# A mixture-of-experts stage kept in slot order: the finish stage removed, its norm moved into the expert loop, and the routing done in batches

## The reference

```python
scores = jax.nn.sigmoid((t @ router_w).astype(jnp.float32))
biased = (scores + router_bias).reshape(-1, 4, 4)          # 4 groups of 4 experts
group_score = jnp.sum(lax.top_k(biased, 2)[0], axis=-1)
sel_group = jnp.argmax(group_score, axis=-1)               # one group a token
_, local_idx = lax.top_k(in_group, 2)                      # two experts in that group
gate = gate / jnp.sum(gate, axis=-1, keepdims=True)
for e in range(16):
    h = jax.nn.silu(t @ w_gate[e]) * (t @ w_up[e])         # 1024 -> 256
    y = y + combine[:, e:e + 1] * (h @ w_down[e])          # 256 -> 1024
x = layer_norm(alpha * x + y, ln_moe_g, ln_moe_b)          # alpha = 2 ** 0.25
```

## Time and profile before

| | us |
|---|---|
| median of 3 runs (lowest, highest) | 1128.58 (1125.63, 1130.79) |
| the profiled execution | 1127.5 |
| its span, first to last instruction | 1125.7 |
| PE busy | 986.8 (88%) |
| DVE busy | 531.6 (47%) |
| ACT busy | 368.3 (33%) |
| POOL busy | 183.5 (16%) |

### The profile page before, as it was taken

One profiled execution on the slowest core, in us unless ns is written; L12 is line 12 of the kernel. 1 busy time (PEld: TensorE's weight loads), 2 busy tenths in 40 slices (PEclk: granted clock), 3 DMA queues, 4 the chain that ended last, 5 costly groups with the idle time before them and its releaser, 6 DMA issues. The chain is left out here.

```text
span 1125.7 us, 15349 instructions
## 1 busy us (share of the span) xinstructions
PE 986.8 (88%) x5513; PEld 843.3 (75%) x5513; DVE 531.6 (47%) x1056; ACT 368.3 (33%) x717; POOL 183.5 (16%) x242
## 2 busy tenths in 40 slices
PE   7999999998999997999999999824999999999700
PEld 6898786766778876888768888724999999999600
DVE  6724513776666655455535454561332333323138
ACT  5112212434443435010132333201355443553331
POOL 0022100211000000112100000002233232332246
PEclk9999999998999999999999999955999999999955
DMA  8102010003500003602300000037698898988376
GB/s 313 55 29 75 1 57 1 1 1 141 235 1 1 1 1 141 232 1 75 101 15 19 20 20 38 38 96 228 191 273 275 253 280 264 282 280 236 56 146 190
DMA packets 57734, 131.24 MB, mean 117 GB/s; under 512 B 8912, under 2 KB 11216, under 8 KB 57680
## 3 DMA queue, kind: packets, MB, share of 16 engines
q1 hardware_dynamic: 49360, 100.95, 26.0%
q0 software_dynamic: 8320, 29.56, 11.7%
HBM read 103.14 MB, written 27.34 MB: 116 GB/s over the span
## 5 line engine op out<-in xcount | busy, mean ns | idle before, releaser
L1606 PE MATMUL h_ps<-xgT,e_gate_up 128*128 128x192 f32 x1024 | 172.0, 330 | 2.1 <-DVE xgT L1681 2.1
L1606 PEld LDWEIGHTS h_ps<-xgT,e_gate_up 128*128 128x128 f32 x1024 | 170.1, 193 | 3.4 <-issue 2.3
L238 PE MATMUL unit_ps<-whi,xhi 128*128 128x512 f32 (+1 forms) x256 | 98.1, 383 | 9.5 <-DVE wlo L269 9.5
L239 PE MATMUL unit_ps<-wlo,xhi 128*128 128x512 f32 (+1 forms) x256 | 97.7, 382 | 0.0
L240 PE MATMUL unit_ps<-whi,xlo 128*128 128x512 f32 (+1 forms) x256 | 97.5, 381 | 0.0
L719 PEld LDWEIGHTS o_ps<-mla_v,prob_T 128*128 128x128 f32 x576 | 72.1, 195 | 15.6 <-issue 10.6
L1691 DVE TENSOR_TENSOR e_dn_lo<-e_dn_raw,e_dn_hi 128x512 fp32r<-128x512 f32 x64 | 39.9, 686 | 84.7 <-ACT e_dn_hi L1641 58.7
L698 PE MATMUL s_ps<-mla_kT,mla_qT 96*128 96x512 f32 (+3 forms) x192 | 73.2, 507 | 3.4 <-PEq L1990 3.4
L719 PE MATMUL o_ps<-mla_v,prob_T 128*128 128x64 f32 x576 | 72.0, 276 | 2.9 <-ACT prob_T L754 2.7
L238 PEld LDWEIGHTS unit_ps<-whi,xhi 128*128 128x128 f32 x256 | 48.4, 189 | 17.9 <-DVE xlo L308 7.3
L240 PEld LDWEIGHTS unit_ps<-whi,xlo 128*128 128x128 f32 x256 | 48.5, 189 | 7.8
(11 more groups left out here) (293 smaller groups left out, 1884.6 us busy)
## 6 DMA issues: line engine op xcount, KB each, us to landing
e_gate_up<-w_gu SPq DMA_DIRECT2D x128, 256.0 KB
e_dn_raw<-w_dn SPq DMA_DIRECT2D x64, 256.0 KB, 5.1
wraw<-w_in SPq DMA_DIRECT2D x24, 256.0 KB, 4.7
y_rows<-zeros SPq DMA_DIRECT2D x10, 512.0 KB, 14.7
xraw<-xT SPq DMA_DIRECT2D x8, 512.0 KB, 6.9
w_out_raw<-w_out SPq DMA_DIRECT2D x8, 512.0 KB, 6.5
x<-x SPq DMA_DIRECT2D x8, 512.0 KB, 6.6
x_rows<-x SPq DMA_DIRECT2D x8, 512.0 KB, 2.6
```

The lines of the kernel that those rows point to most:

```text
L238: pe.matmul(o, hi, whi[:, s, 0:w], start=(s == 0), stop=False)
L239: pe.matmul(o, hi, wlo[:, s, 0:w], start=False, stop=False)
L1606: end = pe.matmul(o, gate_up[:, b, s, w], xT[:, s, :], start=(s == 0), stop=(s == GU - 1))
```

## The change

- A slot is a place in one table of 16 x 192 rows: the expert in the order in which they run, and the token's number in it. The experts run in another order (`RUN`): the first of each of the four groups, then the second of each, and so on. A token's two experts are in one group, so their steps lie at least four apart.
- Routing moves into `cross_attend`, in three batches of tiles: 0 to 3, 4 and 5, 6 and 7 (`rank_experts`, `choose`, `place`, `number`). The sigmoid becomes an exponential on ACT (L1228) and add and reciprocal on DVE. The second set of matmuls is gone. `describe` makes for every slot a weight (already divided by alpha), the token's other slot and the token's number.
- POOL scatters each tile's rows twice, to both slots of a token, into `xs_dram` (16 indirect DMAs, `scatter`, L1442), and at the head of `experts` 16 small ones of 16 bytes a row into `info_dram` (L1574). SP then loads the rows of an expert as one plain piece of the table (`fetch`), two steps ahead, then the slots' data (`info`) and the gains; DVE waits for the gains and POOL's constants before it begins its first step (`consts_made`, `gains_loaded`).
- In a step DVE makes `z = weight * result + row` out of PSUM with the row sum (L1750). SP stores z in slot order in `z_dram`. For a token's second slot, POOL has first gathered the first slot's z over the row (`gather_low`, L1597; lists entries out of bounds are skipped). Mean, the sum of squares (ACT, L1712), 1/sqrt (POOL, L1617) and the norm (DVE, L1760 and, in the next step, `put_out`, L1729) follow in the loop, and POOL scatters finished rows straight to the output (L1620), then waits until they have landed before it goes on.
- The transposed rows are copied by ACT alone (L1681, L1682), and the weights are loaded in one DMA for each of the two kinds. Experts 0 and 1 have their gate and up weights, and expert 0 its down weights, loaded in `cross_attend`.
- `attend` now writes 25.2 MB of zeros (two tables of 3072 rows). `route` and `finish` are gone; `overflow` norms and stores by itself when it runs.

```diff
+SLOTS = NE * CAP
+RUN = [g * EG + e for e in range(EG) for g in range(NG)]
 ...
-            for t in range(NT + 2):
-                sp.dma_start(k.y_dram[t * P:(t + 1) * P, :], zeros[:, 0:D]).then_inc(k.rows_zeroed, 16)
+            for t in range(SLOTS // P):
+                sp.dma_start(k.xs_dram[t * P:(t + 1) * P, :], zeros[:]).then_inc(k.rows_zeroed, 16)
+                sp.dma_start(k.z_dram[t * P:(t + 1) * P, :], zeros[:]).then_inc(k.rows_zeroed, 16)
 ...
     cross_attend, DVE:
+                if t == NT:
+                    choose(0)
 ...
+                if t == NT:
+                    number(0)
                 if t:
                     residual(t - 1)
+                if t == NT - 1:
+                    rank_experts(0)
-            copy_logits(NT - 2)
             norm(NT - 1)
-            copy_logits(NT - 1)
+            rank_experts(1)
+            choose(1)
+            rank_experts(2)
+            number(1)
+            choose(2)
+            number(2)
+            for n in range(3):
+                describe(n)
 ...
     cross_attend, POOL, after the last tile's 1/sqrt:
+            def scatter(n):
+                pool.wait_ge(slots_made, n + 1)
+                for t in range(*BATCHES[n]):
+                    for j in range(2):
+                        pool.indirect_dma_start(k.xs_dram, IndirectOffsetOnAxis(ap=k.slot[:, t, j:j + 1], axis=0), x1[:, t, :], None, ...)
 ...
     experts, SP:
+            sp.wait_ge(k.rows_scattered, 16 * 2 * NT)
+            for e in range(2):
+                fetch(e * CAP, e)
+            sp.wait_ge(k.info_scattered, 16 * 2 * NT)
+            for c in range(2):
+                sp.dma_start(info[0:ROWS[c], :, c, :], slots[c * P:c * P + ROWS[c]]).then_inc(info_loaded, 16)
+            sp.dma_start(g[:], over(A["ln_moe_g"], [P, D])).then_inc(k.gains_loaded, 16)
 ...
+                hold(z_stored, n(32, 128))
+                for c in range(2):
+                    hold(z_made, n(4, 2 * c + 6))
+                    sp.dma_start(k.z_dram[bass.ds(n(CAP, c * P), ROWS[c]), :], z[c][:]).then_inc(z_stored, 16)
+                if not isinstance(e, int):
+                    fetch(n(CAP, 2 * CAP), b)
 ...
     experts, POOL, a step:
-                for c, (_, rows) in enumerate(blocks):
-                    hold(y_taken, n(4, 2 * c + 6))
-                    pool.indirect_dma_start(k.y_dram, ..., yo[c][...], None, compute_op=ALU.add).then_inc(y_added, 16)
-                pool.wait_ge(y_added, n(32, 32))
+                if not last:
+                    hold(z_made, n(4, 4))
+                    read_info(n(1, 1), 1 - b)
+                    hold(ids_read, n(1, 2))
+                    hold(z_stored, n(32, 64))
+                    hold(rows_t, n(1, 2))
+                    gather_low(1 - b)
+                hold(squared, n(2, 2))
+                pool.tensor_scalar(sq[:], sq[:], 1.0 / D, EPS / ALPHA ** 2, ALU.mult, ALU.add)
+                hold(out_made, n(2, 2))
+                pool.tensor_tensor(rs[:], sq[:], half[:], ALU.pow).then_inc(rstd_made, 1)
+                for c in range(2):
+                    hold(out_made, n(2, c + 3))
+                    pool.indirect_dma_start(A["out"], ..., o[c][:], None, ...).then_inc(out_scattered, 16)
+                hold(out_scattered, n(32, 32))
+                pool.sem_inc(out_free, 1)
 ...
     experts, DVE, a step, after h and its low part:
+                put_out(n)          # waits rstd_made and out_free; o = tmp * rs + b
+                dve.wait_ge(low_gathered[b], h(32, 32))
+                dve.wait_ge(z_stored, n(32, 128))
+                for u, (c, j) in enumerate(UNITS):
+                    dve.wait_ge(ysum, n(4, u + 9))
+                    dve.scalar_tensor_tensor(z[c][:, f], yps[r, BANK[u], :], wgt[...], rows[b][c][:, f], ALU.mult, ALU.add,
+                                             accum_out=zsum[r, c, j:j + 1]).then_inc(z_made, 1)
+                # two means, two of tmp = (z - mean) * g, then the next expert's low parts
```

More of the change, by code:

```diff
@@ new lines, in cross_attend @@
+    st = at("ln2_st", 201.5, [P, 2, 6])
+    mv = at("ln2_mv", 201.625, [P, 2, 2])
+    rs = at("ln2_rs", 201.75, [P, 2])
+    half = at("ln2_half", 201.875, [P, 1])
+    nmx = at("xneg_max", 202, [P, XH])
+    rsum = at("xrow_sum", 202.0625, [P, XH])
+    rinv = at("xrow_inv", 202.125, [P, XH])
+    rb = at("router_bias", 24, [P, NE])
+    ones = at("ones", 24.25, [P, P], bf16)
+    tri = at("up_to", 24.5, [P, P], bf16)
+    neg_exp = at("neg_exp", 24.75, [P, NT, NE])
+    score = at("score", 25.25, [P, NT, NE])
@@ L1102, in logits, with place @@
                 last.then_inc(logit, 1)
+            def place(n):
+                lo, hi = BATCHES[n]
+                pe.wait_ge(chosen, n + 1)
+                if n == 0:
+                    pe.wait_ge(consts_made, 3)
+                    pe.wait_ge(exps, XH * NT)
+                o = sps[:, n % 2, 0:NE * (hi - lo)]
+                last = pe.matmul(o, tri[:], sel_b[:, lo:hi, :].rearrange("p t e -> p (t e)"), start=True, stop=(hi == 1))
+                for t in range(hi - 1):
+                    first = max(t + 1, lo)
+                    last = pe.matmul(sps[:, n % 2, NE * (first - lo):NE * (hi - lo)], ones[:],
+                                     over(sel_b[:, t:t + 1, :], [P, hi - first, NE]), start=False, stop=(t == hi - 2))
+                last.then_inc(placed, 1)
             def outputs(t):
@@ L1149, in _ @@
                 logits(t)
+            place(1)
+            place(2)
+            pe.wait_ge(ov_made, 1)
+            pe.matmul(ops[0:1, 0:1], ovsum[:], ones[:, 0:1], start=True, stop=True).then_inc(ov_sum, 1)
         @block.scalar
@@ L1230, in norm, with rank_of @@
                 dve.wait_ge(x2_made, t + 1)
-            def copy_logits(t):
-                dve.wait_ge(logit, t + 1)
-                dve.tensor_copy(k.logits[:, t, :], qps[:, 0:NE]).then_inc(lg_copied, 1)
+            def rank_of(out, b, v):
+                n = v.shape[1]
+                for j in range(4):
+                    if j < 3:
+                        last = dve.tensor_tensor(b[:, j, :, j + 1:4], over(v[:, :, j:j + 1], [P, n, 3 - j]), v[:, :, j + 1:4], ALU.is_ge)
+                    if j:
+                        last = dve.tensor_tensor(b[:, j, :, 0:j], over(v[:, :, j:j + 1], [P, n, j]), v[:, :, 0:j], ALU.is_gt)
+                link(last)
+                link(dve.tensor_reduce(out, b.rearrange("p j n i -> p n i j"), AX.X, ALU.add))
@@ new lines, in experts @@
+    rows = [[at(f"x_rows{b}{c}", 44 + 8 * c + 4 * b, [ROWS[c], D]) for c in range(2)] for b in range(2)]
+    z = [at(f"z{c}", 60 + 4 * c, [ROWS[c], D]) for c in range(2)]
+    tmp = [at(f"ln3_tmp{c}", 68 + 4 * c, [ROWS[c], D]) for c in range(2)]
+    o = [at(f"ln3_out{c}", 76 + 4 * c, [ROWS[c], D]) for c in range(2)]
+    junk = at("ln3_junk", 84, [P, D])
+    g = at("ln3_g", 97, [P, D])
+    b_ = at("ln3_b", 101, [P, D])
+    gate_up, dn_raw = k.e_gu, k.e_dn
+    xT = at("xgT", 137, [P, KD, CAP])
@@ L1489, in experts @@
+    half = at("minus_half", 149.6875, [P, 2])
+    share = at("minus_share", 149.71875, [P, 1])
     ident = cst[:, C_ID:C_ID + P]
[L1490 to L1492 removed]
+    info_i = info[:].bitcast(i32)
+    gu_loaded, dn_loaded = k.gu_loaded, k.dn_loaded
     rows_loaded = [k.sem("rows_loaded_even"), k.sem("rows_loaded_odd")]
[L1494 removed]
@@ new lines, in _ @@
+            pool.wait_ge(consts_made, 1)
+            pool.memset(sq[:], float(D)).then_inc(consts_made, 1)
+            pool.memset(zsum[:], 0.0).then_inc(consts_made, 1)
+            pool.memset(half[:], -0.5).then_inc(consts_made, 1)
+            pool.memset(share[:], -1.0 / D).then_inc(consts_made, 1)
+            pool.memset(rs[:], 1.0).then_inc(consts_made, 1)
+            for c in range(2):
+                pool.memset(tmp[c][:], 0.0).then_inc(consts_made, 1)
+            pool.wait_ge(consts_made, 8)
@@ L1600, in step @@
                     for gu in range(2):
-                        o = hps[:, m, gu * CAP:(gu + 1) * CAP]
                         w = slice(gu * DE + m * P, gu * DE + (m + 1) * P)
-                        for s in range(GU):
-                            if m == 0 and gu == 0:
-                                pe.wait_ge(gu_loaded[b][s], h(16, 16))
-                            end = pe.matmul(o, gate_up[:, b, s, w], xT[:, s, :], start=(s == 0), stop=(s == GU - 1))
+                        for s in range(KD):
+                            end = pe.matmul(hps[:, m, gu * CAP:(gu + 1) * CAP], gate_up[:, b, s, w], xT[:, s, :], start=(s == 0), stop=(s == KD - 1))
                     end.then_inc(gsum, 1)
```

720 lines of the change are left out of this document (320 added, 400 removed).

## The result

| | before | after |
|---|---|---|
| median (lowest, highest), 4 runs each | 1127.11 (1125.18, 1130.79) | 1090.47 (1087.68, 1094.19) |
| ratio, 95% interval | | 0.9673 (0.9633 to 0.9714) |
| the profiled execution, its span | 1127.5, 1125.7 | 1087.68, 1085.8 |
| mean granted clock | 0.940 | 0.959 |

The changed kernel is faster by 36.6 us. The forecast of the median was 1083, so 7.5 us of the expected 44.1 didn't come; 1090.47 lies in the range. The forecast was made against a profiled execution, and against that it was 1083.4: the profiled execution of after is 4.3 above it. Part of the rest is chance: this execution is the fastest of the four.

A forecast was written before the change was run, and what follows sets the result against it. PE bounds the expert steps (17.60 of 17.60 us) and idles in the finish stage. End -43.3, start -0.8, steps 0 sum to -44.1: span 1081.6, with 1.8 around it 1083.4, predicted 1083, range 1072 to 1118.

The forecast's parts named there:

- The end: After the last matmul: the finish stage goes (-48.9 us), the tail grows, worth -43.3 us, bounds -40 to -45.
- The start: From routing to the first expert step's end: worth -0.8 us, bounds -8 to about +14.
- two paths: From routing to the first result, rows and slot data with the gains; the later one counts.
- The path of rows: At the start: routing, 16 full scatters, row loads, transposes and copies; gate and up matmuls start at 772, not 779.59.
- the second path: At the start: 16 small scatters landed at 781.4, then slots' data and gains at 790; down matmuls near 792.
- the forecast's wait at the shared bank: First step: DVE runs two full-width operations before emptying PSUM, so PE waits; step ends at 799.5 instead of 800.25.
- The steps: Expert steps: PE's 17.60 us stay if nobody comes later; 0 for 15 steps, bounds 0 and +32.
- GpSimd's ring: Expert steps: POOL's loop from output half over scatters, landing, lists, gather, variance and power to the next, 15.6 us.
- rivals 1 and 4: Expert steps: 1, POOL's ring exceeds PE's step, +15 to +32, chance 0.15; 4, DVE holds up POOL, +85, chance 0.06.
- Rival 4's rule: Expert steps: each of six POOL operations waits one full-width DVE operation (1.28 us), ring 23.3 us; chance 0.06.
- rival 2: Expert steps: DMA becomes the bound, 5.24 MB at 279 GB/s take 18.8 us, +18, 1101; chance 0.07.
- rival 3: At the start: indirect DMAs cost POOL as much to issue as adding scatters, +14 to +15, 1098; chance 0.12.

The follow-up runs named there:

- the step with four clears: The changed kernel with four clears of a scratch tile on POOL before the power in every step: 1117.74 us, ratio 0.9901.

## Why the prediction was right

**The end: right, its last term by luck.** 48.9 removed, confirmed by taking that stage alone away (48.3). The tail was worked out at 8.4 us from the last product to the second scatter and measured 8.7; from there to the end 11.5 was forecast and 11.0 measured. Together 19.9 and 19.7. But the 11.5 were 5.5 for the landing and 6 for the rest, and they measured 2.2 and 8.8, of which POOL's drain is 6.60: two errors that cancel.

**The start: the mechanism right, the size off by 2.8.** The forecast had two paths and said that the gains' load is the later one. It is: DVE's first h waits for `ln_b`. The path of rows came within a microsecond (772 forecast, 771.38 measured), and routing's last slots at 752 were made at 749.16. On the second path two terms were mis-sized. The barrier: POOL began its small scatters at 762.50, 6.2 us after its last big one, where I had 0.8 from the last scatter's issue; this put the landing of the second gain at 793.6 instead of 790. POOL's drain at the end of `cross_attend` ends only at 760.45, 4.1 after that scatter, and all engines wait for it. And the down matmuls started 3 us later than 792, at 794.96. The second step began at 802.26, for 799.5. The 7.5 us between the two came out as 7.3, but not by the forecast's wait at the shared bank: PE doesn't wait there in this step (DVE's first `z` waits 1.41 for PE), and its second to ninth down matmuls start 0.43 us apart, the later ones 0.23, at a granted clock of 0.75 over the stretch. That is 1.7 us over before's 5.6, and in no term of the forecast. Price of the second path as shown by removing it: nothing clear for the gains alone, 5.1 us in the trace and 6.9 in the median with the gather behind it. I had named the gather nowhere as a gate, and with the gains out of the way it was one.

**The steps: 0 forecast, 1.6 measured.** Fourteen periods take 247.05 for 246.26 (0.8; thirteen are 17.64 and one 17.73, for 17.59), and a last step that waits 0.53 for `z` at the bank ends 16.8 after its gate and up start where before it took 16.0 (0.8). The 0.05 us a step remain without the norm's operations, so they are no wait for the norm; what they are stays open.

**GpSimd's ring (rivals 1 and 4): rightly held unlikely, with more luck than the sum shows.** 15.6 was worked out, and the step with four clears leaves 15.57, but that agreement is luck: the ring that binds there goes over DVE's run and the copy held beside it, not over a landing of 7.3. The prediction had put a held-up POOL operation at one full-width operation each. It can be held for several: 3.68 us over half of `ln_tmp` and all of `e_dn_lo`; so it is in three steps of the loop (3.65 to 3.68), in four more it is 2.4 to 3.5, in the rest 0.5 to 1.4, as the landing comes later (up to 7.5 us from issue to the copy). Rival 4's rule was right in kind and its count wrong: one operation in a step is held for long, not six; the others run in 0.2 to 1.2 us.

**DMA (rival 2): not the bound.** 4.5 and 4.8 MB in two steps (253 and 273 GB/s over 17.6), 5.24 worked out, at 0.76 and 0.86 of the engines' time. The zeros were hidden, as counted: the last tile's 1/sqrt ends at 731.49, before at 731.30.

**Issue cost (rival 3): rightly set aside.** The 32 scatters went at 1.27 us each (0.97 and 0.30), but for the first with 2.01 and one of the small ones with 1.50.

So the forecast was 4.3 us short in its own execution: start 2.8, steps 1.6, tail 0.3, end -0.5.

## What to carry to other kernels

A stage behind the last product costs its whole length, and its work can vanish into a loop that one engine bounds, if that loop's other rings stay shorter than its step: work out each ring with its landings, test the sum by adding a known delay, and look in the trace which ring took it. A sum that fitted to 0.03 us was here that of another ring. Where a change starts a new phase, list all loads and gathers that its first step waits for and order them by when they are needed, each in its queue: here 5 to 7 us lay in two that were in the wrong place. The next gate stood right behind the one removed, and the load moved ahead made late what had stood there. Read an edit's worth in the trace from an event just ahead of it, for the executions differed by up to 4.5 us before the edits began.
